# Attention scores: the rotary high-by-low product on 64 rows of TensorE, heads taken in pairs

## What is computed

```python
s = (jnp.einsum('bqhr,bkr->bhqk', q_abs, ckv).astype(jnp.float32)
     + jnp.einsum('bqhp,bkp->bhqk', q_r, kr).astype(jnp.float32)) * SOFTMAX_SCALE
s = jnp.where(mask[None, None], s, NEG_INF)
p = jax.nn.softmax(s, axis=-1).astype(ckv.dtype)
return jnp.einsum('bhqk,bkr->bqhr', p, ckv)
```

## Time and profile before

| | us |
|---|---|
| median of 3 runs | 2369.53 (2368.09 to 2371.31) |
| profiled execution, its own time | 2361.09 |
| span in the profile | 2359.2 |
| TensorE busy | 2211.8 (94%) |
| VectorE busy | 1312.7 (56%) |
| ScalarE busy | 1014.4 (43%) |
| GpSimd busy | 367.7 (16%) |

### The profile page before, as it was taken

How to read it: one execution, slowest core, us unless ns; L and a number is a source line. 1 busy time by engine, 2 the same in 40 slices (tenths; PEclk the granted TensorE clock), 3 DMA queues, 4 the chain that set the end, 5 groups by cost and what they waited for, 6 DMA issues and landing times.

```text
span 2359.2 us, 36115 instructions
## 1 busy us (share of the span) xinstructions
PE 2211.8 (94%) x12021; PEld 2042.9 (87%) x12021; DVE 1312.7 (56%) x2647; ACT 1014.4 (43%) x1811; POOL 367.7 (16%) x500
## 2 busy tenths in 40 slices
PE   5999599999999997976999999999999999999997
PEld 4888578888888886856999999989999899999997
DVE  4665477788777774414643364445634464446435
ACT  3554366555555544414433353335323443344333
POOL 1333221011100010104200140005000410023001
PEclk9999699999999999998999999999999999999999
DMA  4444431110100010405453445343444235333433
GB/s 172 162 155 149 110 81 51 44 37 28 38 21 23 19 63 10 161 2 190 137 174 108 137 127 174 117 137 111 153 145 144 97 131 174 113 131 130 177 119 130
DMA packets 134880, 258.20 MB, mean 109 GB/s; under 512 B 18682, under 2 KB 84482, under 8 KB 133430
## 3 DMA queue, kind: packets, MB, share of 16 engines
q1 hardware_dynamic: 111454, 223.29, 28.8%
q10 hardware_dynamic: 20960, 20.19, 2.9%
q0 software_dynamic: 2304, 12.58, 1.4%
HBM read 213.45 MB, written 42.79 MB: 109 GB/s over the span
## 4 chain that ended last, share of the span: by engine, by line
PE 46%; POOL 3%; issue 2%; DVE 2%; ACT 1%; DMA 1%; POOLq 0%; SPq 0%; DVEq 0%; ACTq 0%
PE d_ps L112 46%; POOL d_win L1411 1%; PE d_ps L1567 1%; DMA d_hf<-out_ht 0%; POOL d_fstat L1389 0%; ACT d_wr L1288 0%; POOLq L96 0%; DMA d_gfin<-in_g_final 0%; POOL d_win L1424 0%; ACT d_mrg L1347 0%; DVE d_gate_p L1518 0%; ACT L1335 0%; POOL d_ols L80 0%; DVE d_wr L80 0%; POOL d_fstat L1392 0%
## 5 line engine op out<-in xcount | busy, mean ns | idle before, releaser
L112 PE MATMUL d_ps<-d_ht,d_wr 128*128 128x412 f32 x3840 | 746.3, 353 | 36.3 <-DVE d_ht L80 21.5
L112 PEld LDWEIGHTS d_ps<-d_ht,d_wr 128*128 128x128 f32 x3840 | 726.9, 191 | 41.4 <-DVE d_ht L80 21.6
L80 DVE TENSOR_TENSOR d_wr<-d_ws,d_wr 128x1024 fp32r<-128x1024 f32 x262 | 324.1, 1237 | 569.0 <-ACT d_wr L1288 568.8
L1288 ACT ACTIVATE d_wr<-d_ws 128x1024 fp32r<-128x1024 f32 x262 | 277.4, 1059 | 576.9 <-PE d_ps L112 574.5
L842 PE MATMUL b_ps<-kt,b_qs 128*128 128x512 f32 (+3 forms) x1600 | 359.8, 377 | 17.5 <-POOL b_qs L80 14.0
L842 PEld LDWEIGHTS b_ps<-kt,b_qs 128*128 128x128 f32 x1600 | 278.3, 195 | 64.3 <-POOL b_qs L80 14.4
L861 PE MATMUL b_ps<-b_pt,kv 128*128 128x512 f32 x816 | 210.3, 400 | 8.8 <-DVE b_pt L80 8.7
L80 DVE TENSOR_TENSOR b_pt<-b_ps,b_pt 128x512 fp32r<-128x512 f32 x272 | 172.0, 683 | 81.3 <-ACT b_pt L746 80.9
L739 ACT ACTIVATE b_p<-b_p,b_bias 128x1024 f32<-128x1024 f32 (+7 forms) x192 | 171.9, 898 | 104.0 <-DVE b_low L797 100.5
L746 ACT ACTIVATE b_pt<-b_ps 128x512 fp32r<-128x512 f32 x272 | 143.8, 596 | 146.2 <-PE b_ps L852 145.8
L861 PEld LDWEIGHTS b_ps<-b_pt,kv 128*128 128x128 f32 x816 | 152.5, 190 | 48.1 <-DVE b_pt L80 14.1
(11 more groups left out here) (194 smaller groups left out, 2299.1 us busy)
## 6 DMA issues: line engine op xcount, KB each, us to landing
d_ws<-in_w SPq DMA_DIRECT2D x264, 512.0 KB, 3.3
out_q<-a_qout SPq DMA_DIRECT2D x17, 768.0 KB, 3.3
d_hf<-out_ht SPq DMA_DIRECT2D x26, 412.0 KB, 3.6
a_x<-in_x ACTq DMA_DIRECT2D x17, 512.0 KB, 3.6
out_ht<-a_hf SPq DMA_DIRECT2D x17, 512.0 KB, 4.1
d_olf<-out_olat SPq DMA_DIRECT2D x42, 206.0 KB, 3.0
b_qf<-out_q SPq DMA_DIRECT2D x32, 256.0 KB, 2.8
b_qf<-out_q SPq DMA_DIRECT2D x128, 64.0 KB, 2.6
```

The source lines that it names most:

```text
L80: return e.tensor_tensor(low, source, high.bitcast(f32), ALU.subtract)
L112: mm = pe.matmul(out, stationary(a, k), moving(b, k), start=first and k == 0 and a + b == 0, stop=last and k == depth - 1 and a == 1)
L1288: act.activation(wr[k % 2][:, 0, :, :], ws[k % 4][:, :, :], ACT.Copy).then_inc(w_hi, 1)
```

## The change

Scores are made for two heads at a time. The order of S steps becomes: for each pair of heads, for each chunk, the even head and then the odd head. The first four products of a head are as before. The fifth, high x low of the rotary part, runs over 64 rows only: for even heads over partitions 0 to 63, where their high part is, for odd heads over partitions 64 to 127. So for odd heads GpSimd now puts the low part on partitions 0 to 63 and leaves the high part on 64 to 127. Low x low is no longer computed. The even head's fifth product is held back and issued just ahead of the odd head's, and both signal `s_ok`. C of either head therefore waits for the pair, as does the C in the planner, where an odd S costs five units and an even one four.

```diff
-    scores = [("S", u, h, c) for u in range(units) for h in range(HG) for c in range(chunks(u))]
+    scores = [("S", u, pair + side, c) for u in range(units) for pair in range(0, HG, 2) for c in range(chunks(u))
+              for side in range(2)]
...
-            return 5 * max(0.107, 0.0535 * width(u, step[3], 4))
+            return (4 + step[2] % 2) * max(0.107, 0.0535 * width(u, step[3], 4))
...
-            out = [("S", u, *at)]
+            out = [("S", u, at[0] | 1, at[1])]
...
-                split(pool, qs[u % 2][ROPE:P, 2, :, :], qf[u % 2][ROPE:P, 1, :, :],
-                      qs[u % 2][ROPE:P, 2, :, :]).then_inc(q_ok, 1)
+                split(pool, qs[u % 2][ROPE:P, 2, 0:HG:2, :], qf[u % 2][ROPE:P, 1, 0:HG:2, :],
+                      qs[u % 2][ROPE:P, 2, 0:HG:2, :])
+                split(pool, qs[u % 2][0:ROPE, 2, 1:HG:2, :], qf[u % 2][0:ROPE, 1, 1:HG:2, :],
+                      qs[u % 2][0:ROPE, 2, 1:HG:2, :]).then_inc(q_ok, 1)
...
-                    dve.wait_ge(s_ok, n + 1)
+                    dve.wait_ge(s_ok, number["S", u, h | 1, c] + 1)
...
-                    pairs = ((0, 0), (0, 2), (1, 0), (2, 1), (2, 3))
+                    pairs = ((0, 0), (0, 2), (1, 0), (2, 1))
                     for k, (a, b) in enumerate(pairs):
-                        mm = pe.matmul(ps_s[n % NS][:, 0:keys * P], q[:, a, h, :], kt[:, first:first + keys, b, :],
-                                       start=k == 0, stop=k == len(pairs) - 1)
-                    mm.then_inc(s_ok, 1)
+                        pe.matmul(ps_s[n % NS][:, 0:keys * P], q[:, a, h, :], kt[:, first:first + keys, b, :],
+                                  start=k == 0, stop=False)
+                    rows = slice(ROPE * (h % 2), ROPE * (h % 2) + ROPE)
+                    low_keys = (ps_s[n % NS][:, 0:keys * P], q[rows, 2, h, :], kt[rows, first:first + keys, 3, :])
+                    if h % 2 == 0:
+                        lower = low_keys
+                    else:
+                        pe.matmul(*lower, start=False, stop=True).then_inc(s_ok, 1)
+                        pe.matmul(*low_keys, start=False, stop=True).then_inc(s_ok, 1)
```

## The result

The changed kernel takes 2403.97 us (median of 4 runs, 2400.54 to 2404.86) against 2369.73 for the kernel before: a ratio of 1.0142, 95% interval 1.0124 to 1.0159, 34 us slower. The forecast was 2418, slower.

A forecast was written before the change was run, and what follows sets the result against it. TensorE's row of matmuls was taken to bound attention. Crossings less overlap +39, evictions +8 and small terms +2 gave +49 us on the 2369.5 median: 2418 us, range 2372 to 2450.

The forecast's parts named there:

- Crossings and overlap: Attention scores on TensorE: switching between 128 and 64 rows costs 72 us, side-by-side products save 33: +39 us.
- The terms 0.09 + 0.10 on each side: Score pairs: going to 64 rows and coming back each lose 0.09 us, plus 0.10 for an exposed weight load.
- The second load's 0.07: Score pairs: the odd head's 64-row product starts 0.07 us after the even head's, behind its load.
- Evictions and tail: Attention: lost eviction slack costs 0.05 us per pair, 8 us; two exponentials at the stage's end cost 2.3 us.
- The other step that failed: The sum for attention: 39 + 8 + 2 = +49 us, its costs simply added.
- two exponentials ahead of the last transposes: End of attention: the third head's two exponentials now also follow the last score pair, 2.3 us, ends 0 and 4.
- GpSimd: Low-half preparation: two 64x256 pieces cost one 64x512 plus a start, mostly hidden; 0.2 us in all.
- (b): Score pairs: row-height switches cost time and the two products run one after the other; +68, 2437 us; 25 in 100.
- (a): Score pairs: the two products overlap and 64 rows cost no switch; -22, 2348 us; 12 in 100.
- (c): Score pairs: switches of 0.09 us with loads hidden, or products neither waiting nor overlapping; first form +12, 2382 us; 13 in 100.
- (d): Score bank ring: each odd step finds VectorE busy, evictions cost +48 not 8; about +90, 2459 us; 8 in 100.

The follow-up runs named there:

- the runs for rows, 96 included: Kernel before, no pairs, every step's fifth product on 64 rows: ratio 1.0459; the same edit on 96 rows: 1.0002.
- the pairs with full rows: Changed kernel with its fifth products over all 128 rows again, pairs and joint evictions kept: ratio 1.0072 to the kernel before.
- the price told: Changed kernel with the planner counting 0.38 us more for an odd step: ratio 1.0130 to the kernel before.
- the last run: Changed kernel with 64-row products only for 512-key chunks and the planner counting 0.38 us more per odd step: 1.0072 to the kernel before.

## Why the prediction was right, and where its sum was off

The direction and the mechanism held: the crossing has the two parts that the earlier trace rows show, in a case (128 to 64 rows) that no row of before had. The Trainium skill's rule ("TensorEngine Tiling (Array Packing)", Key Properties) agrees with the runs for rows, 96 included: its list of tiling modes (Available Configurations) has 128, 64 and 32 rows and no 96. Term by term:

- **Crossings and overlap, forecast +39.** The terms 0.09 + 0.10 on each side were right to a hundredth. The second load's 0.07 was mis-sized: it is nothing, since loads for different rows run side by side as the products do. The two loads of the earlier trace rows, 0.07 apart, went to the same rows, so they were the wrong neighbour. The Trainium skill's figure of about 4 ns ("TensorE: Matmul & The Clock Gate", Part 3) was nearer than my row. With 0.38 in place of 0.45 a pair, TensorE's row grows by 61 - 33 = 28 us. Run alone, full width showed 0.39 a visit and all widths together 106.6 / 320 = 0.33.
- **Evictions and tail, forecast +8 and +2.3.** Order and joint eviction together cost 15.8 us when they stand alone, so 10.3 was too low; the order of the steps, 8.6 us by itself, had no term at all in the forecast. The other step that failed is the one that treated these costs as a sum with the crossings: 28 + 15.8 would be 44, and 34.2 was measured. The change over the pairs with full rows is 721.3 - 702.9 = 18.4 us only. Some 5 us of the missing 10 are TensorE's waits that shrink when the crossings come (45.9 to 40.8 us in the matmul queue). The lone 64-row products, too, lost less than the visits add up to. Where the rest goes is not shown.
- **The tail by itself.** I had priced two exponentials ahead of the last transposes, 2.3 us. Where the planner's list leaves as many key tiles after the scores as before, the tail is longer by just that (2.3 with the price told, 2.4 in the last run). In the change the list leaves ten to twelve more, each group of three about 0.9 us dearer than between scores, and I had not looked at the new list.
- **GpSimd, forecast +0.2.** Two pieces of 64x256 take 799 ns each where one of 64x512 took 1384, 0.2 us more a unit, hidden from the third unit on:

```profile
L80 POOL TENSOR_TENSOR b_qs<-b_qf,b_qs 64x256 fp32r<-64x256 f32 x64 | 51.1, 799 | 4.4
```

Of the rivals, (b) is out: the starts coincide, and taking the overlap away cost 32.6 us. The run that is built as (b) has it, both products on the same rows, lost 66.8 us in attention, and (b) was priced at 68. (a) and the cheap crossing of (c) are out by the timeline. (d) would have needed the pairs with full rows to lose 50 us or more; they lost 17. The forecast of +49 against +34 is therefore 11 us of a second load that isn't there and 10 of costs that don't add, less 5 to 6 by which the pairing (8 + 2.3 forecast, 15.8 measured alone) was set too low. That the total came as near as it did is partly luck, since these errors stand against each other.

## What to carry to other kernels

Count the visits to a divided array, not the rows saved. Here one visit costs 0.38 us, and a second product of 512 columns running beside the first gives back 0.23, so by these numbers, as an estimate, a visit has to hold two such pairs before it pays (none here did, and that wasn't tried); a product of 64 rows that stands alone among full ones is better run on 96 or 128. Where an engine is full, price each change of order by an experiment that keeps the order and takes the rest away: run alone, the pairing lost 16 us of attention, where the change lost 34. And when an edit changes what the planner is told, look at the list it makes: here it moved 12 us of work behind the last score.

## What was unexpected

- Weight loads of the two halves start together (0.00 to 0.01 us apart) and cost one exposed load, not two.
- Costs that stand one behind the other on TensorE and VectorE overlap: crossings +28 by the timeline's spacings, pairing alone +16, both +34.
- Decode took one of two courses, and the record sorts them by chip, not by the attention ahead of it. From its first to its last matmul it takes 112 to 114 us in the profile of the kernel before and in all eight profiles from the two chips where the unchanged kernel had medians of 2359.15 and 2362.3 us. It takes 122 us in both profiles from the third chip, where that median was 2372.4, and in the profile of the change. In the longer course TensorE stands still once for 4 to 5 us while the caches are being fetched, and the matmuls after it are slower:

```profile
988.98 0.38 PE L1036 MATMUL c_ps<-ident,e_rn 128*128 128x128 f32 x2
993.38 1.54 PE L1017 MATMUL c_ps<-c_ckeys,e_qp 128*64 128x512 f32 x3 [4.02 <-issue]
994.72 1.48 PE L1021 MATMUL c_ps<-c_rkeys,e_qp 128*64 128x256 f32 x6
```

  The same six products of line 1021 take 0.85 us elsewhere in that stage. The granted clock is 1.00 up to the standstill and 0.50, the lower of its two levels, from 993.3 to 995.9. The 10 us may be what lies between the profiled execution of before (2361.1) and its median (2369.5), but the chips of these two are not on record and there is no profile of a longer execution of before, so that stays open.
